# A triangular inverse inside a two-layer transformer kernel: levels 1 to 4 on compact 32-column blocks, four TensorE tiles at a time

## The chip, the cores and the metric

The kernel runs on one core of one Trainium2 chip, in one launch. The metric is the time of a whole execution on the device in microseconds (us), as the median of several runs; lower is better.

## The reference, cut to what matters

The program computes two layers of a 1024-wide transformer block on 256 tokens (a gated delta rule beside latent attention, feed-forwards), and behind it two layers of other mixers and feed-forwards. The change touches one step of the gated delta rule. Each layer has 8 heads of 128 channels, and a head's 256 tokens are cut into chunks:

```python
CHUNK = 64
m = jnp.where(strict, jnp.einsum('nbhid,nbhjd->nbhij', kb, kc) * decay, 0.0)
eye = jnp.eye(CHUNK, dtype=f32)
t_inv = lax.linalg.triangular_solve(eye + m, jnp.broadcast_to(eye, m.shape), left_side=True, lower=True)
u = t_inv @ (vc * bc[..., None])
w = t_inv @ (kb * jnp.exp(gcum)[..., None])
```

`m` is strictly lower triangular, so `eye + m` has an inverse that can be built from small blocks on the diagonal upwards. The kernel works on chunks of 128 tokens, not 64, which gives the same result: two chunks for each head, and so 16 inverses of 128 x 128 for each layer. All numbers are float32.

## The kernel before, in words

**Where the inverse stands.** `delta_rule` handles the heads in two groups `g` of four; with two chunks each, a group has 8 independent *units* `u`, all of which go through the inverse together. There are two groups for each of two layers, so `inverse(g, fill)` (L1026) is run four times in an execution: it begins at about 353, 422, 1176 and 1246 us. VectorE (DVE) first makes `MT`, the transposed and decayed product of keys with keys for the 8 units.

**The doubling.** `TI` holds the inverse of the blocks on the diagonal so far and `TTI` its transpose. At the start the blocks are 2 x 2 (`TTI = I - EBS[0]`, L2343). Level s (1 to 5) doubles the block's size. `EBS[s % 2]` is `MT` times a mask that leaves just the new off-diagonal blocks, with sign. TensorE forms X = EBS TI in banks 0 and 1 of PSUM; X is copied to `XB`; then `TTI X` and `X TTI` are *added* to the copies of TI and TTI that stay in PSUM (banks 2 and 3, banks 4 and 5; `start=False`), and both are copied out again. The last step (L1075 and `last_block`, L1085) joins the two 64 x 64 halves.

**Tiles.** All products of the five levels are done by `square_products` (L1028) as 64 x 64 x 64: unit u, rows 0 to 63 (`BLOCKS[0]`, low) and rows 64 to 127 (`BLOCKS[1]`, high) are two matmuls, on two tiles of the array with 64 rows and 64 columns each. A profile shows each float32 matmul as two weight loads and two matmul records, and those of two neighbouring tiles alternate. So 8 units x 2 halves are 32 records.

**Who copies.** ScalarE (ACT) copies the low half (L1484), DVE the high half (L2348), 64 partitions x 512 in one instruction. DVE also makes the mask product for the next level (L2355, 128 x 1024). In the first group of each layer DVE does a convolution between (L2030, L2034) and ACT a SiLU (L1418).

**Filler.** While ACT and DVE copy, TensorE must not stand still. `mixer_filler` (L963) hands out the tiles of large independent projections: `MIX_FILL` says how many tiles (of 128 x 128 weights and 256 columns, two records each, L976) stand at each point of the order. The points `ti0`, `level01` to `level05` are those of group 0, `ti1`, `level11` to `level15` of group 1. Sixteen tiles are a *job*, whose two outputs ACT moves from PSUM (`move`, L1422 to L1432) once TensorE has done the job's last tile. Within a level the order on TensorE is: wait, X (32 records), filler, wait, TTI X (32), X TTI (32), and then the next level's wait. The order on each engine is the program's order, and all waits are semaphores counted (`cnt.next`): `products_for_act` and `products_for_dve` from TensorE, `operands_of_act` and `operands_of_dve` to it. Between the first products and level 1 stand the products of keys and queries (L1051) and DVE's `QK` (L2352).

**Constants.** `kst` holds masks, seven of them of 128 columns for the levels. All but its first 128 columns are loaded once, behind the ninth weight slab.

Of the kernel before, what the change touches and what calls it, by code (L numbers as in the profile page):

```python
# [24 lines left out]
ALU = mybir.AluOpType  # L25
ACT = mybir.ActivationFunctionType
AXX = mybir.AxisListType.X

P = 128
# [18 lines left out]
MIX_FILL = dict(keys_early=3, keys=21, queries=14, decay0=24, ti0=1, level01=10, level02=10, level03=5, level04=5,  # L48
                level05=5, rb0=6, u00=5, state0=3, carry0=5, u10=3, decay1=26, ti1=1, level11=6, level12=6, level13=6,
                level14=6, level15=6, rb1=6, u01=5, state1=3, carry1=5, u11=3, out=9,  # L50
# [21 lines left out]
def ada_turns():  # L72
# [26 lines left out]
_CK = dict(ones=128, ident=128, cmask=512, bmask=512, upper=128, levels=7 * 128, rot=128, pick=128,  # L99
           freq=1)  # L100
# [29 lines left out]
CK, NK = columns(_CK)  # L130
# [25 lines left out]
def build(nc, wstream, astream, crow, xT, memT, pos, par1, par2, pars, const, outT):  # L156
    ctx = ExitStack()
    with ctx:
# [11 lines left out]
        kst = sb("kst", [P, NK])  # L170
# [24 lines left out]
        level = [kst[:, CK["levels"][0] + P * s:CK["levels"][0] + P * (s + 1)] for s in range(7)]  # L195
# [40 lines left out]
        TMP = 14336  # L236
# [5 lines left out]
        EBS = [area(TMP + 4096, 8, P), area(TMP + 9216, 8, P)]  # L242
# [62 lines left out]
        BLOCKS = (slice(0, 64), slice(64, P))  # L305

        def blocks_of(b, rows):

            return psum[rows, b].rearrange("p (u t) -> p u t", t=64)

# [200 lines left out]
        def _(pe):  # L511
# [514 lines left out]
            def inverse(g, fill):  # L1026

                def square_products(bank, lhs, rhs, blocks=(0, 1), signals=(products_for_act, products_for_dve), **flags):  # L1028
                    for u in range(8):
                        for r in blocks:  # L1030
                            rows = BLOCKS[r]
                            mm = pe.matmul(psum[rows, bank + r, 64 * u:64 * u + 64], lhsT=lhs(rows, u), rhs=rhs(rows, u),  # L1032
                                           skip_group_check=True, **{n: f(u) for n, f in flags.items()})
                            if u == 7:
                                mm.then_inc(signals[r], 1)

                def own(v):
                    return lambda rows, u: v[rows, u, rows]

                def unit(rows, u):  # L1040
                    return ident[rows, rows]

                opens = dict(start=lambda u: u == 0, stop=lambda u: False)
                adds = dict(start=lambda u: False, stop=lambda u: False)
                alone = dict(start=lambda u: True, stop=lambda u: True)

                pe.wait_ge(operands_of_dve, cnt.next("operands_of_dve"))
                square_products(2, own(TTI), unit, **opens)
                for u in range(8):
                    j, c = u // 2, u % 2  # L1050
                    mm = pe.matmul(psum[:, u // 4, u % 4 * P:(u % 4 + 1) * P],  # L1051
                                   lhsT=qkv[:, 8 + 4 * g + j, c * P:(c + 1) * P],
                                   rhs=qkv[:, 4 * g + j, c * P:(c + 1) * P], start=True, stop=True)
                mm.then_inc(products_for_dve, 1)
                for u in range(8):
                    for r, rows in enumerate(BLOCKS):
                        pe.matmul(psum[rows, 4 + r, 64 * u:64 * u + 64], lhsT=unit(rows, u), rhs=TTI[rows, u, rows],
                                  start=u == 0, stop=False, skip_group_check=True)
                fill(f"ti{g}")

                for s in range(1, 6):
                    pe.wait_ge(operands_of_act, cnt.next("operands_of_act"))
                    pe.wait_ge(operands_of_dve, cnt.next("operands_of_dve", 2 if s == 1 else 1))
                    square_products(0, own(EBS[s % 2]), own(TI), **alone)
                    fill(f"level{g}{s}")
                    pe.wait_ge(operands_of_act, cnt.next("operands_of_act", 1 if s == 1 else 2))
                    pe.wait_ge(operands_of_dve, cnt.next("operands_of_dve", 1 if s == 1 else 2))
                    square_products(2, own(TTI), own(XB), (0, 1) if s < 5 else (0,), **adds)
                    square_products(4, own(XB), own(TTI), **adds)

                pe.wait_ge(operands_of_act, cnt.next("operands_of_act"))
                pe.wait_ge(operands_of_dve, cnt.next("operands_of_dve"))
                low, high = BLOCKS
                for u in range(8):
                    mm = pe.matmul(psum[high, 3, 64 * u:64 * u + 64], lhsT=EBS[0][low, u, high], rhs=TI[low, u, low],  # L1075
                                   start=True, stop=True)
                mm.then_inc(products_for_act, 1)
# [209 lines left out]
        def _(act):  # L1287
# [114 lines left out]
            def mixer(layer):  # L1402
# [70 lines left out]
                for g in range(2):  # L1473
                    act.wait_ge(inputs_for_act, cnt.next("inputs_for_act"))
                    E(DT, DT, ACT.Exp)
                    E(eg, rows4[g][:, :, P:T], ACT.Exp).then_inc(functions_for_dve, 1)
                    move(f"decay{g}")
                    if g == 0:
                        silu(9)
                    low, high = BLOCKS  # L1480

                    def take(dst, bank, rows):
                        act.wait_ge(products_for_act, cnt.next("products_for_act"))
                        E(dst, blocks_of(bank, rows), ACT.Identity).then_inc(operands_of_act, 1)  # L1484

                    take(TI[low, :, low], 2, low)
                    move(f"ti{g}")
                    for s in range(1, 6):
                        take(XB[low, :, low], 0, low)
                        if g == 0 and s in (2, 3):  # L1490
                            silu(8 + s)
                        move(f"level{g}{s}")
                        take(TI[low, :, low], 2, low)
                        take(TTI[low, :, low], 4, low)
                    take(XB[high, :, low], 3, high)
# [149 lines left out]
        def _(dve):  # L1645
# [655 lines left out]
            def delta_rule(layer):  # L2301
# [3 lines left out]
                def lev(s):  # L2305
                    return level[s].unsqueeze(1).broadcast_to((P, 8, P))
# [7 lines left out]
                def product():  # L2314
                    dve.wait_ge(products_for_dve, cnt.next("products_for_dve"))

                convolve(layer, 8)
                for g in range(2):
# [21 lines left out]
                    TT(EBS[0], MT, lev(0), ALU.mult)  # L2340
                    D()
                    TT(TTI, I8, EBS[0], ALU.subtract).then_inc(operands_of_dve, 1)
                    TT(EBS[1], MT, lev(1), ALU.mult)  # L2343
                    low, high = BLOCKS

                    def take(dst, bank, rows):
                        product()
                        return V.tensor_copy(dst, blocks_of(bank, rows))  # L2348

                    take(TI[high, :, high], 3, high).then_inc(operands_of_dve, 1)  # L2350
                    product()
                    TT(QK, two(0), DT, ALU.mult).then_inc(operands_of_dve, 1)  # L2352
                    for s in range(1, 6):
                        take(XB[high, :, high], 1, high).then_inc(operands_of_dve, 1)
                        last = TT(EBS[(s + 1) % 2], MT, lev(s + 1), ALU.mult)  # L2355
                        if g == 0 and s in (1, 2):
                            convolve(layer, 9 + s)
                        if s < 5:
                            take(TI[high, :, high], 3, high).then_inc(operands_of_dve, 1)
                        else:  # L2360
                            last.then_inc(operands_of_dve, 1)
                        take(TTI[high, :, high], 5, high).then_inc(operands_of_dve, 1)
                    take(TTI[low, :, high], 4, low)
# [542 lines left out]
def constants():  # L2906
# [6 lines left out]
    levels = []  # L2913
    for s in range(7):
        b = 2 << s
        new = (i[:, None] // b == i[None, :] // b) & (i[None, :] % b >= b // 2) & (i[:, None] % b < b // 2)
        levels.append(np.where(new, -1.0 if s else 1.0, 0.0))
    rot = np.zeros((P, P))
    for m in range(P):
        if m % 64 < 32:  # L2920
            rot[m + 32, m] = -1.0
        else:
# [4 lines left out]
                          i[None, :] >= i[:, None], *levels, rot, pick, freq[:, None]], 1).astype(np.float32)  # L2927
# [18 lines left out]
```

## Time and profile before

| | |
|---|---|
| median of 3 runs | 2652.08 us (2651.91 to 2652.47) |
| profiled execution, its own time | 2653.67 us |
| span of the profiled execution | 2651.5 us |
| mean granted TensorE clock | 0.997 of full speed |
| busy share: TensorE, DVE, ACT, GpSimd | 99%, 60%, 17%, 6% |
| matmul records of the four inverses (64*64) | 2176 of 17960 |

The span runs from the first to the last instruction; the execution's own time is about 2 us longer. A matmul's record lasts from its start to the modelled end, some 0.2 us of which overlap with those behind it, so a group's busy time says less than the distance between starts.

### The profile page before, as it was taken

Reading aid. Unit: us, or ns where it says so; the run is one execution under the profiler, and the core shown is the slowest. Engines: PE = TensorE matmul, PEld = TensorE weight load, DVE = VectorE, ACT = ScalarE, POOL = GpSimd, SP = SyncE. Lnnn points to the kernel's source line nnn. Section 1 sums busy time; section 2 is a strip of 40 time slices with the busy share of each in tenths; the row PEclk is TensorE's granted clock in tenths of the full one; section 3 lists DMA queues with packets and bytes.
Section 4 is the critical chain, followed back from the end, with each engine's and each line's share of the span. In section 5 each row is a group of like instructions: output and inputs, shape, how many; then the busy total and the mean of one; then the engine's idle time right before and its main releaser. Section 6 shows DMA issues by size and latency. Waiting matters only on the chain.

```text
span 2651.5 us, 43071 instructions
## 1 busy us (share of the span) xinstructions
PE 2613.9 (99%) x17960; PEld 2360.4 (89%) x17960; DVE 1595.2 (60%) x3378; ACT 446.9 (17%) x857; POOL 160.3 (6%) x138
## 2 busy tenths in 40 slices
PE   9999999999999999999999999999999999999998
PEld 8899888788999999888878999987889998888998
DVE  4587675646677778675554666344358752324775
ACT  1011333221000100233321100013110011211000
POOL 0000000000330430000000330000000000000000
PEclk9999999999999999999999999999999999999999
DMA  9887422527446556532345444443344444343442
GB/s 379 307 334 268 163 104 81 198 96 244 170 160 253 200 207 223 214 128 81 141 154 199 155 164 175 151 166 112 111 144 158 159 160 177 116 143 120 158 154 94
DMA packets 74450, 458.88 MB, mean 173 GB/s; under 512 B 8308, under 2 KB 9216, under 8 KB 28176
## 3 DMA queue, kind: packets, MB, share of 16 engines
q1 hardware_dynamic: 73120, 449.28, 46.3%
q0 software_dynamic: 1136, 6.86, 0.7%
q8 instruction: 141, 2.31, 0.3%
q14 instruction: 53, 0.43, 0.1%
HBM read 455.01 MB, written 1.09 MB: 172 GB/s over the span
## 4 chain that ended last, share of the span: by engine, by line
PE 94%; DVE 4%; DMA 1%; DVEq 1%; issue 0%; ACT 0%; ACTq 0%
PE psum L548 20%; PE psum L780 14%; PE psum L722 14%; PE psum L629 9%; PE psum L976 8%; PE psum L828 4%; PE psum L1032 3%; PE psum L605 2%; PE psum L735 2%; PE psum L664 2%; PE psum L996 2%; PE psum L651 2%; PE psum L924 1%; PE psum L951 1%; DMA aring<-astream 1%; DVE aring L1912 1%
## 5 line engine op out<-in xcount | busy, mean ns | idle before, releaser
L548 PE MATMUL psum<-h,ring 128*128 128x256 f32 x1536 | 335.0, 379 | 1.4 <-DVE arena L1886 0.8
L548 PEld LDWEIGHTS psum<-h,ring 128*128 128x128 f32 x1536 | 291.1, 190 | 43.1 <-ACT arena L1460 1.7
L780 PE MATMUL psum<-arena 128*128 128x128 f32 x2112 | 249.7, 275 | 1.2 <-DVE arena L1786 1.2
L780 PEld LDWEIGHTS psum<-arena 128*128 128x128 f32 x2112 | 242.6, 192 | 1.4 <-DVE arena L1786 1.4
L629 PE MATMUL psum<-aring,ring 128*128 128x256 f32 x1088 | 237.3, 379 | 1.7 <-issue 1.7
L976 PE MATMUL psum<-h,ring 128*128 128x256 f32 x1024 | 235.4, 383 | 0.0
L629 PEld LDWEIGHTS psum<-aring,ring 128*128 128x128 f32 x1088 | 205.8, 190 | 29.9 <-issue 2.4
L976 PEld LDWEIGHTS psum<-h,ring 128*128 128x128 f32 x1024 | 189.9, 190 | 30.2 <-issue 4.9
L780 PE MATMUL psum<-arena,ring 128*128 128x128 f32 x1584 | 191.6, 275 | 0.0
L780 PEld LDWEIGHTS psum<-arena,ring 128*128 128x128 f32 x1584 | 184.3, 192 | 0.2
L722 PE MATMUL psum<-arena 128*128 128x128 f32 x1440 | 170.6, 275 | 0.0
L722 PEld LDWEIGHTS psum<-arena 128*128 128x128 f32 x1440 | 165.6, 192 | 0.0
L548 PE MATMUL psum<-arena,ring 128*128 128x256 f32 x720 | 157.9, 380 | 1.0 <-DVE arena L2148 1.0
L1912 DVE SCALAR_TENSOR_TENSOR aring<-aring,condb 128x1024 f32<-128x1024 f32 x128 | 153.0, 1220 | 8.5 <-DMA aring<-astream 7.7
L548 PEld LDWEIGHTS psum<-arena,ring 128*128 128x128 f32 x720 | 136.1, 190 | 24.3 <-issue 4.7
L1300 ACT ACTIVATE sq<-x 128x512 f32<-128x512 f32 x48 | 30.3, 631 | 591.8 <-DVEq L1889 381.7
L722 PE MATMUL psum<-h,ring 128*128 128x128 f32 x960 | 117.0, 275 | 0.0
L477 POOL TENSOR_TENSOR arena<-ring 128x512 f32<-128x512 f32 x60 | 77.1, 1285 | 645.2 <-PE psum L584 426.3
L722 PEld LDWEIGHTS psum<-h,ring 128*128 128x128 f32 x960 | 112.2, 192 | 0.2
L664 PE MATMUL psum<-h,ring 128*128 128x256 f32 x448 | 96.9, 379 | 0.3 <-DVE arena L1972 0.3
L664 PEld LDWEIGHTS psum<-h,ring 128*128 128x128 f32 x448 | 85.0, 190 | 12.2 <-issue 0.6
L1783 DVE TENSOR_TENSOR arena<-ring 128x512 f32<-128x512 f32 x66 | 45.6, 691 | 75.4 <-PE psum L780 74.3
(463 smaller groups left out, 3726.0 us busy)
## 6 DMA issues: line engine op xcount, KB each, us to landing
ring<-wstream SPq DMA_DIRECT2D x349, 1024.0 KB, 4.9
aring<-astream SPq DMA_DIRECT2D x128, 512.0 KB, 4.9
arena<-astream SPq DMA_DIRECT2D x16, 512.0 KB, 18.3
arena<-wstream SPq DMA_DIRECT2D x3, 1024.0 KB, 20.2
arena<-decays POOLq DMA_DIRECT2D x2, 1024.0 KB, 5.4
sq<-decays POOLq DMA_DIRECT2D x2, 1024.0 KB, 4.7
kst<-const SPq DMA_DIRECT2D x1, 1216.5 KB, 7.6
x<-xT SPq DMA_DIRECT2D x1, 1024.0 KB, 4.9
```

The costliest lines, as they stand in the source:

```text
L477: nc.gpsimd.tensor_tensor(new[:, 0], w[:, 2], w[:, 3], ALU.add)
L548: mm = pe.matmul(out, lhsT=tile_at(at[0] % RING, t), rhs=rhs(k), start=k == 0, stop=k == kt - 1)
L605: mm = pe.matmul(psum[:, bank + bk, c * P:(c + 1) * P], lhsT=w, rhs=v, start=m == 0 and name in ("M1", "M5"), stop=m == 3, skip_group_chec ...
L629: mm = pe.matmul(psum[:, s % 4, n * T:(n + 1) * T], lhsT=tile_at(slot, 8 * n + 4 * (k % 2) + k // 2), rhs=rhs(k), start=k == 0, stop=k == ...
L651: mm = pe.matmul(psum[:, s, n * T:(n + 1) * T], lhsT=slab[:, t * P:(t + 1) * P], rhs=h[:, k], start=k == 0 and n == 0, stop=k == KD - 1, s ...
L664: mm = pe.matmul(psum[:, s % 4, n * T:(n + 1) * T], lhsT=tile_at(at[0] % RING, n * KD + k), rhs=h[:, k], start=k == 0, stop=k == KD - 1)
L722: mm = pe.matmul(out, lhsT=w, rhs=v, start=m == 0 and name in ("M1", "M5"), stop=m == 3, skip_group_check=True)
L780: mm = pe.matmul(out, lhsT=w, rhs=v, start=m == 0 and name in ("M1", "M5", "M3", "M4"), stop=m == NF // 2 - 1, skip_group_check=True)
L828: mm = pe.matmul(psum[:, memory_bank(kind, job), a * T:(a + 1) * T], lhsT=w, rhs=v, start=k == 0, stop=k == KD - 1)
L976: mm = pe.matmul(psum[:, 6 + job % 2, n * T:(n + 1) * T], lhsT=tile_at(i % RING, f % TPS), rhs=h[:, k], start=k == 0, stop=k == KD - 1)
L1032: mm = pe.matmul(psum[rows, bank + r, 64 * u:64 * u + 64], lhsT=lhs(rows, u), rhs=rhs(rows, u), skip_group_check=True, **{n: f(u) for n, f ...
L1912: STT(out=w, in0=w, scalar=1.0, in1=condb[:], op0=ALU.mult, op1=ALU.mult, accum_out=sums[:, b:b + 1]).then_inc(ada_used, 1)
```

## The change

The inverse's blocks are held compactly, and a matmul makes 32 columns instead of 64. `QUADS` are the four groups of 32 partitions. The four diagonal 32 x 32 blocks of a unit stand one below the other in a 128 x 32 area (`TC` for TI, `XC` for X). A product takes 64 rows of weights and of data (`BLOCKS[b // 2]`) and 32 columns of weights (`QUADS[b]`), on a tile of 64 rows and 32 columns; one of its two 32-row halves is zero in one operand. Four such tiles stand side by side in the array, so a product of all units is 8 x 4 = 32 matmuls, 64 records, where it was 32 records.

- Levels 1 to 4 (which build blocks of up to 32 x 32) use this form. `NEAR` (`MT` within blocks of 32, negated) is made once; the mask of a level is applied when X is copied, by DVE, in two instructions of 64 x 256 (`level[s - 1]`).
- Level 5 joins 32 x 32 blocks with tiles of 32 rows and 32 columns, straight from `MT`, 16 matmuls and then 24; the last two joins keep their 64 x 64 form.
- ACT copies TC for both halves (two instructions of 64 x 256) and TTI for two of the four blocks (two of 32 x 256); DVE copies TTI for the other two.
- Each level's `TTI X` and `X TTI` are now followed by a filler point of its own, `turn`, of one tile in levels 1 to 4. The order of a level is: wait, X (64 records), filler `level`, wait, TTI X (64), X TTI (64), filler `turn`. The filler tiles of a group's inverse add up to the same as before (36 and 31).
- `kst` shrinks by 480 columns.

```diff
-MIX_FILL = dict(keys_early=3, keys=21, queries=14, decay0=24, ti0=1, level01=10, level02=10, level03=5, level04=5,
-                level05=5, rb0=6, ..., decay1=26, ti1=1, level11=6, level12=6, level13=6,
-                level14=6, level15=6, rb1=6, ...
+MIX_FILL = dict(keys_early=3, keys=21, queries=14, decay0=24, ti0=1, level01=8, turn01=1, level02=8, turn02=1, level03=7, turn03=1,
+                level04=6, turn04=1, level05=2, rb0=6, ..., decay1=26, ti1=1, level11=7, turn11=1, level12=6, turn12=1, level13=6, turn13=1, level14=5,
+                turn14=1, level15=2, rb1=6, ...
-                def square_products(bank, lhs, rhs, blocks=(0, 1), signals=(products_for_act, products_for_dve), **flags):
+                def quad_products(bank, lhs, rhs, signals, start, stop):
                     for u in range(8):
-                        for r in blocks:
-                            rows = BLOCKS[r]
-                            mm = pe.matmul(psum[rows, bank + r, 64 * u:64 * u + 64], lhsT=lhs(rows, u), rhs=rhs(rows, u),
...
+                        for b in range(4):
+                            mm = pe.matmul(psum[QUADS[b], bank + b // 2, 32 * u:32 * u + 32], lhsT=lhs(b, u),
+                                           rhs=rhs(b, u), start=start(u), stop=stop, skip_group_check=True)
+                            if u == 7 and b in signals:
+                                mm.then_inc(signals[b], 1)
...
                 pe.wait_ge(operands_of_dve, cnt.next("operands_of_dve"))
-                square_products(2, own(TTI), unit, **opens)
+                quad_products(2, own(TTI), units, {3: products_for_act}, lambda u: u == 0, False)
...
+                quad_products(4, units, own(TTI), {}, lambda u: u == 0, False)
+                fill(f"ti{g}")
+
+                for s in range(1, 5):
+                    pe.wait_ge(operands_of_act, cnt.next("operands_of_act"))
+                    if s == 1:
+                        pe.wait_ge(operands_of_dve, cnt.next("operands_of_dve"))
+                    quad_products(0, own(NEAR), compact(TC), {3: products_for_dve}, lambda u: True, True)
+                    fill(f"level{g}{s}")
+                    if s > 1:
+                        pe.wait_ge(operands_of_act, cnt.next("operands_of_act"))
+                    pe.wait_ge(operands_of_dve, cnt.next("operands_of_dve", 1 if s == 1 else 2))
+                    quad_products(2, own(TTI), compact(XC), {3: products_for_act}, lambda u: False, False)
+                    quad_products(4, compact(XC), own(TTI), {1: products_for_act, 3: products_for_dve}, lambda u: False, False)
+                    fill(f"turn{g}{s}")
...
+                fill(f"level{g}5")
+                pe.wait_ge(operands_of_act, cnt.next("operands_of_act", 2))
+                pe.wait_ge(operands_of_dve, cnt.next("operands_of_dve", 2))
+                for u in range(8):
+                    out = slice(256 + 32 * u, 288 + 32 * u)
+                    for r in range(2):
+                        even, odd = QUADS[2 * r], QUADS[2 * r + 1]
+                        if r == 0:
+                            mm = pe.matmul(psum[odd, 2, out], lhsT=TTI[odd, u, odd], rhs=XC[odd, u], start=True, stop=True,
+                                           skip_group_check=True)
...
+                        mm = pe.matmul(psum[even, 4 + r, out], lhsT=XC[odd, u], rhs=TTI[odd, u, odd], start=True,
+                                       stop=True, skip_group_check=True)
...
+                    for s in range(5):
+                        if s == 4:
+                            take((TQ[QUADS[0], :, 0:32], quads_of(2, QUADS[0])), (TQ[QUADS[1], :, 32:64], quads_of(2, QUADS[1])),
+                                 (TC[QUADS[2]], quads_of(3, QUADS[2])))
+                        else:
+                            take(*[(TC[rows], quads_of(2 + r, rows)) for r, rows in enumerate(BLOCKS)])
+                        if s > 0:
+                            take(own(0), own(1))
...
+                    for s in range(1, 5):
+                        product()
+                        for r, rows in enumerate(BLOCKS):
+                            last = TT(XC[rows], quads_of(r, rows), all_units(level[s - 1][rows]), ALU.mult)
+                        last.then_inc(operands_of_dve, 1)
                         if g == 0 and s in (1, 2):
                             convolve(layer, 9 + s)
...
+                        product()
+                        for b in (2, 3):
+                            last = V.tensor_copy(TTI[QUADS[b], :, QUADS[b]], quads_of(5, QUADS[b]))
+                        last.then_inc(operands_of_dve, 1)
```

## Rows read from the trace of the kernel before

**Rows 1.** The page: busy time of the engines; the chain that ended last, by engine.

```profile
PE 2613.9 (99%) x17960; PEld 2360.4 (89%) x17960; DVE 1595.2 (60%) x3378; ACT 446.9 (17%) x857; POOL 160.3 (6%) x138
...
PE 94%; DVE 4%; DMA 1%; DVEq 1%; issue 0%; ACT 0%; ACTq 0%
```

**Rows 2.** Busy time by stretch: the first two inverses; then clock, DMA share, GB/s.

```profile
352.61:390.01 37.40, 37.40 (x633) 32.84 (x632) 24.10 (x37) 12.27 (x21) 0.00 (x0) 1.00 0.23 81
421.78:457.02 35.24, 35.24 (x623) 30.94 (x622) 17.77 (x21) 10.63 (x18) 0.00 (x0) 1.00 0.23 80
```

**Rows 3.** The critical chain through the first inverse: start us, us, what.

```profile
352.68 1.08 PE psum L1032 x32
353.76 1.98 PE psum L1051 x16
...
356.82 0.63 PE psum L976 x2
...
363.04 3.14 PE psum L1032 x96
366.18 4.51 PE psum L976 x20
...
387.19 1.95 PE psum L1032 x47
389.13 0.95 PE psum L1075 x16
...
395.40 0.89 PE psum L1116 x8
```

**Rows 4.** Timeline: X of level 3 to level 4, with ACT's and DVE's copies.

```profile
376.12 3.21 PE L1032 MATMUL psum<-arena 64*64 64x64 f32 x96
377.30 0.59 ACT L1484 ACTIVATE arena<-psum 64x512 f32<-64x512 f32 x1 [2.35 <-PE psum L1032]
...
378.28 0.69 DVE L2348 COPY arena<-psum 64x512 f32<-64x512 f32 x1 [0.24 <-PE psum L1032]
379.26 2.02 PEld L976 LDWEIGHTS psum<-h,ring 128*128 128x128 f32 x10
```

**Rows 5.** Timeline: the first four, then eight weight loads of four 32-column tiles (L843).

```profile
305.32 0.13 PEld L843 LDWEIGHTS psum<-sq,kst 128*32 128x32 f32 x4 [0.33 <-DVE sq L2225]
305.32 0.64 PE L843 MATMUL psum<-sq,kst 128*32 128x512 f32 x4
...
305.32 0.16 PEld L843 LDWEIGHTS psum<-sq,kst 128*32 128x32 f32 x8 [0.33 <-DVE sq L2225]
...
305.32 1.07 PE L843 MATMUL psum<-sq,kst 128*32 128x512 f32 x8
```

**Rows 6.** Line L843 from 305 to 306.5 us: ns min/median/max, first and last start.

```profile
L843 PEld LDWEIGHTS psum<-sq,kst x8: 106/108/109, 305.3 to 305.4; 128*32 128x32 f32 x8
L843 PE MATMUL psum<-sq,kst x8: 592/605/617, 305.3 to 305.8; 128*32 128x512 f32 x8
```

**Rows 7.** Timeline: copies, products and a convolution of other sizes on ACT and DVE.

```profile
355.78 1.23 DVE L2352 TENSOR_TENSOR arena<-psum,arena 128x1024 f32<-128x1024 f32 x1 [1.25 <-PE psum L1051]
...
361.15 2.79 DVE L2034 SCALAR_TENSOR_TENSOR arena<-arena,p 128x256 f32<-128x256 f32 x6
...
391.58 1.02 ACT L1497 ACTIVATE arena<-psum 128x1024 f32<-128x1024 f32 x1 [0.87 <-PE psum L1109]
392.50 0.59 ACT L1498 ACTIVATE arena<-psum 128x512 f32<-128x512 f32 x1
```

**Rows 8.** Line L1032 over the whole span: who waited for it (us, times).

```profile
  ACT arena L1484: 95.8, 64
  DVE arena L2348: 55.9, 60
```

More of the change, by code:

```diff
@@ L98 @@
            lq1=64, lk1=64, lq2=64, lk2=64)
-_CK = dict(ones=128, ident=128, cmask=512, bmask=512, upper=128, levels=7 * 128, rot=128, pick=128,
+_CK = dict(ones=128, ident=128, cmask=512, bmask=512, upper=128, pairs=128, near=128, levels=4 * 32, unit=32, rot=128, pick=128,
            freq=1)
@@ L194, in build @@
         ones, ident, upper, rot, pick = K("ones"), K("ident"), K("upper"), K("rot"), K("pick")
-        level = [kst[:, CK["levels"][0] + P * s:CK["levels"][0] + P * (s + 1)] for s in range(7)]
+        level = [kst[:, CK["levels"][0] + 32 * s:CK["levels"][0] + 32 * (s + 1)] for s in range(4)]
         now = [0]
@@ L305, in build, with quads_of @@
         BLOCKS = (slice(0, 64), slice(64, P))
+        QUADS = tuple(slice(32 * b, 32 * b + 32) for b in range(4))
         def blocks_of(b, rows):
             return psum[rows, b].rearrange("p (u t) -> p u t", t=64)
+        def quads_of(b, rows, at=0):
+            return psum[rows, b, at:at + 256].rearrange("p (u t) -> p u t", t=32)
         def bank(b, n=1, w=512):
@@ L1054, in inverse @@
                 mm.then_inc(products_for_dve, 1)
-                for u in range(8):
[L1056 to L1069, printed above, removed]
+                quad_products(4, units, own(TTI), {}, lambda u: u == 0, False)
@@ new lines, in inverse @@
+                pe.wait_ge(operands_of_act, cnt.next("operands_of_act"))
+                for u in range(8):
+                    for r, t in enumerate((TQ[QUADS[0], u, 0:32], TC[QUADS[2], u])):
+                        even, odd = QUADS[2 * r], QUADS[2 * r + 1]
+                        mm = pe.matmul(psum[odd, r, 32 * u:32 * u + 32], lhsT=MT[even, u, odd], rhs=t,
+                                       start=True, stop=True, skip_group_check=True)
+                        if u == 7:
+                            mm.then_inc((products_for_act, products_for_dve)[r], 1)
@@ L1480, in mixer, with take, own @@
                     low, high = BLOCKS
-                    def take(dst, bank, rows):
+                    def take(*parts, scale=1.0):
                         act.wait_ge(products_for_act, cnt.next("products_for_act"))
[L1484 to L1489, printed above, removed]
+                        for dst, src in parts:
+                            last = E(dst, src, ACT.Identity, scale=scale)
+                        last.then_inc(operands_of_act, 1)
+                    def own(b):
+                        return TTI[QUADS[b], :, QUADS[b]], quads_of(4 + b // 2, QUADS[b])
+                    for s in range(5):
[6 more added lines that the diff above has]
+                            take(own(0), own(1))
                         if g == 0 and s in (2, 3):
                             silu(8 + s)
[L1492 to L1495, printed above, removed]
+                        move(f"turn{g}{s}" if s else f"ti{g}")
+                        if s < 4:
+                            move(f"level{g}{s + 1}")
+                    take((XC[QUADS[1]], quads_of(0, QUADS[1])), scale=-1.0)
+                    move(f"level{g}5")
+                    take((TQ[QUADS[1], :, 0:32], quads_of(2, QUADS[1], 256)))
+                    take((TTI[QUADS[0], :, QUADS[1]], quads_of(4, QUADS[0], 256)))
+                    take((XB[high, :, low], blocks_of(3, high)), scale=-1.0)
                     act.wait_ge(products_for_act, cnt.next("products_for_act"))
@@ L2339, in delta_rule @@
                     D()
[L2340 removed]
+                    TT(PAIRS, MT, all_units(K("pairs")), ALU.mult)
                     D()
[L2342 to L2343 removed]
+                    TT(TTI, I8, PAIRS, ALU.subtract).then_inc(operands_of_dve, 1)
+                    TT(NEAR, MT, all_units(K("near")), ALU.mult)
                     low, high = BLOCKS
[L2346 to L2348 removed]
@@ L2364, in delta_rule @@
+                    V.tensor_copy(TTI[low, :, high], blocks_of(4, low))
                     dve.wait_ge(functions_for_dve, cnt.next("functions_for_dve"))
@@ L2912, in constants @@
     never, always = np.full((P, P), NEG), np.zeros((P, P))
-    levels = []
-    for s in range(7):
+    pairs = (i[:, None] // 2 == i[None, :] // 2) & (i[None, :] % 2 == 1) & (i[:, None] % 2 == 0)
+    near = np.where(i[:, None] // 32 == i[None, :] // 32, -1.0, 0.0)
+    levels, q = [], np.arange(32)
+    for s in range(1, 5):
         b = 2 << s
-        new = (i[:, None] // b == i[None, :] // b) & (i[None, :] % b >= b // 2) & (i[:, None] % b < b // 2)
-        levels.append(np.where(new, -1.0 if s else 1.0, 0.0))
+        levels.append((i[:, None] % 32 // b == q[None, :] // b) & (i[:, None] % b >= b // 2) & (q[None, :] % b < b // 2))
+    unit = i[:, None] % 32 == q[None, :]
     rot = np.zeros((P, P))
```

52 lines of the change are left out of this document (25 added, 27 removed).

## The prediction

> **What bounds the kernel now.** I read the page first. TensorE is busy 99% of the span and is 94% of the chain that ended last [rows 1]: the kernel's time is the time of TensorE's stream, and work that leaves DVE or ACT is worth nothing. Then the windows over the inverses: in 352.61 to 390.01 us TensorE is busy all 37.40 us, at granted clock 1.00 (the 2.4 GHz level), DMA at 0.23 of its share [rows 2]. So there is no idle time for the change to remove; it has to make TensorE's own work shorter. The other three inverses are the same pieces with 36 or 31 filler tiles between. Third the chain through the first inverse, piece by piece [rows 3], which gives prices. Fourth the timeline round one level, to see who copies when [rows 4]. Last the one place where this kernel already runs four tiles of 32 columns side by side, L843 [rows 5, 6]. ACT and DVE wait 151.7 us in sum for the inverse's products [rows 8], so they have room.
>
> **Prices on TensorE.** A lone 64 x 64 tile (L1075, one half only) takes 0.95 us for 16 records, 59.4 ns each; a 128 x 128 product with 128 columns (L1116) takes 0.89 / 8 = 111 ns [rows 3]. From 64 to 128 columns of weights and of data the record grows by 52 ns, 0.81 ns for each column. Two tiles together: 32 records in 1.08 us, which is 16 x 59.4 = 0.95 us and 0.13 us before the dense work behind them starts [rows 3]. So two neighbouring tiles run fully in parallel, 29.7 ns a record, and what sets the pace is each tile's own cycle, not the pair. Two dense records take 0.63 us where they stand alone and 4.51 / 20 = 0.226, or by difference (4.51 - 0.63) / 18 = 0.216, in a row [rows 3]: 0.20 us more than 2 x 0.216. A burst of small tiles between dense ones thus costs 0.13 + 0.20 = 0.33 us besides its records. The burst of 96 takes 3.14 us = 48 x 59.4 (2.85) + 0.13 + 0.16: the last 0.16 us is the wait of the next level's X for DVE's copy, which ends at 378.28 + 0.69 [rows 3, 4].
>
> **Before, one inverse.** Its 544 records are 512 in paired tiles (15.2 us) and 32 on a lone tile (1.9 us): 17.1 us. Check: the window 37.40 less L1051 (1.98) less 72 dense records (15.5) leaves 19.9 us; 17.1 + 8 bursts x 0.33 (2.6) + 4 waits x 0.16 (0.6) is 20.3. Good to 0.4 us.
>
> **After, one inverse: what is not shown, and its bounds.** Tiles of 64 rows and 32 columns with 32 columns of data occur nowhere. By the 0.81 ns a column the cycle of one tile is 59.4 - 26 = 33.4 ns. Do four of them run in parallel? L843 says yes for column tiles: the first four loads last 0.13 us in all, the shortest 0.106, so the fourth starts 0.024 us after the first; the eighth ends at 0.16 and lasts 0.109, so it starts at 0.051, 27 ns behind the fourth, its own tile's first [rows 5, 6]. Four loads of 32 columns at once cost the time of one, 27 ns, and the four matmuls start within 0.02 us of each other [rows 5]. Row tiles in parallel are shown by the inverse itself. So I take one *round* of four records at 33.4 ns, 8.4 ns a record; the floor is the 27 ns of the load. The upper bound for a record is what before shows sustained, 29.7 ns.
>
> The records: start 2 x 64, levels 1 to 4 with 4 x 192, level 5 with 32 (two tiles) and 48 (three tiles), together 976; in rounds 32 + 192 + 16 + 16 = 256. 256 x 33.4 ns = 8.55 us, and L1075 as before 0.95: 9.5 us. **Records: 9.5 - 17.1 = -7.6 us.**
>
> **Bursts.** The `turn` points cut each of four bursts in two: 12 for 8. **+4 x 0.33 = +1.3 us.** The filler tiles themselves are the same number.
>
> **Waits.** Level 1's X waits for `QK`: DVE can start it once L1051 is done and needs 1.23 us [rows 7]; TensorE meanwhile does 16 rounds (0.53), a burst's edge and two dense records, 1.3 us: about even, +0.1. After `TTI X` of a level ACT makes two copies of 64 x 256. ACT's slope is (1.02 - 0.59) / 512, 0.84 ns an element [rows 7], so one is 0.59 - 0.22 = 0.37 and, a little overlapped, two are 0.65 to 0.75; with 0.25 for the drain and the semaphores the copy is there 0.9 to 1.0 us after the last record of `TTI X`. TensorE is then at `X TTI` (0.53), one filler tile (0.43) and a burst's edges (0.33): 1.3 us. Covered, also in level 4 with three ACT copies (1.2). The wait of 0.16 us in the four old bursts goes, -0.6. DVE's masked copies, two of 256 elements at about 0.47 (2.79 / 6 [rows 7]), lie under 5 to 8 filler tiles (2.2 us and more); the convolution behind them (2.79 us and a little more [rows 7]) ends about when `turn` starts and is wanted only after it. The mask products L2355 leave DVE, which saves nothing. New and uncovered: in level 5 the last join (L1075's successor) follows directly on the 48 records and waits for ACT's copy of the 32 x 256 block, 0.25 + 0.37 = +0.65. **Waits together: +0.15 us.** If ACT's copy of 256 elements cost as much as one of 512 (0.59), two more waits of 0.2 to 0.4 us would come in every level: a rival below.
>
> **The rest.** 480 fewer constant columns are 0.24 MB less in one transfer while TensorE is busy: nothing. A job's copy by ACT (`move`) now stands once between `TTI X` copies; it falls under the 1.3 us. Behind the inverse nothing changes, and transfers (0.23 of their share) will keep up with a stream that arrives 6 us earlier.
>
> **Sum.** -7.6 + 1.3 + 0.15 = -6.1 us for each of four inverses, -24.5 us. Profiled execution 2653.7 (span 2651.5): 2629. It was 1.6 us above the median of the runs shown, 2652.1, from which I forecast 2627.6, rounded to **2628 us**.
>
> Break-even is where 976 records cost 6.1 us more than at 8.4 ns: 14.6 ns a record.
>
> **Rival 1: the cycle doesn't shrink with the columns.** Then a round of four costs 59.4 ns as a round of two did: 256 x 59.4 ns + 0.95 = 16.2 us, -0.9 + 1.3 + 0.15 = +0.5 us an inverse, +2 us: **2654 us**. For it: no row has so few columns. Against: 111 against 59 ns for half the columns is still nearly in proportion, and loads of 32 columns turn round in 27 ns [rows 3, 5]. Chance 0.12. The Trainium skill has this rule against the change, in "TensorEngine Tiling (Array Packing)", section Instruction Overhead: a matmul carries some 60 cycles, one with a free dimension of 1 takes as long as one of 60, and a tiling factor isn't to be taken from a dimension that is already small. Read as a floor on columns, it gives this rival's time; read as cycles it does not bite if a float32 record takes two cycles a column, which would fit the 0.81 ns a column seen here.
>
> **Rival 2, the other side: the stream of instructions can't keep up.** TensorE must be fed two records (a load and a matmul) every 8.4 ns; before shows 29.7 ns sustained, and only short runs faster: eight loads and four matmuls start within 0.05 us [rows 5]. If the sequencer delivers a pair in, say, 20 ns, 976 x 11.6 ns = +11.3 - 6.1 = +5.2 us an inverse, +21: **2673 us**; at the bound of 29.7 ns it is 4 x (20.8 - 6.1) = +59, 2711 us. It decides above 14.6 ns a record; a queue that runs ahead during the filler would soften it. Against: in bursts of 96 records the two tiles show no sign of starving. Chance 0.15. The Trainium skill ("TensorE: Matmul & The Clock Gate", Part 1) says that starts of matmuls never lie closer than about 25 ns, however few columns; by that the sum would be about +10 us an inverse, 2691 us. Rows 5 contradict it across tiles: four matmuls start within 0.02 us; no row here tells for a long stream.
>
> **Rival 3: new waits eat part.** ACT now has up to five small copies in each `turn`, and TensorE passes from X to copy to X with one filler tile. If small copies cost 0.55 us each instead of 0.37, each turn waits some 0.4 us and level 5 about 0.8 more: 2.5 us an inverse, **2638 us**. For it: fixed costs weigh more in small instructions. Against: the slope above. Chance 0.15.
>
> **Numbers.** The forecast has 0.58. Its own range: rounds at 27 ns give another 4 x 256 x 6.4 ns = -6.6 us, 2621; 10 ns a record gives +6, 2634. Up to the other cases: from 2621 to 2656 lie the forecast, rivals 1 and 3, 0.85 together, less tails of 0.05. Faster by over 0.2% (5.3 us, about what a measurement can tell from no change): forecast and rival 3, 0.73. Rival 1 is within 0.2%: 0.12. Slower is rival 2: 0.15.
>
> **What the profile after would show.** Right: bursts of 64 records in about 0.53 + 0.13 us, of 128 in 1.1 to 1.2; the window of the first inverse about 31.3 us with the same filler; no waits of the small records for ACT before level 2, 3, 4; one of about 0.65 us before the 64 x 64 join. Rival 1: 64 records in 0.95 + 0.13. Rival 2: a burst of 128 that costs far more than twice one of 64, its starts evenly spaced. Rival 3: idle time before the small loads, released by ACT. The prediction would be wrong most of all through the price of a record: every nanosecond on it is 3.9 us.

## The result: slower by 0.38%

| | before | after |
|---|---|---|
| median of 5 runs each | 2652.47 us (2651.91 to 2655.62) | 2663.43 us (2660.77 to 2664.57) |
| profiled execution, its own time | 2653.67 us | 2660.77 us |
| ratio, 95% interval | | 1.0038 (1.0024 to 1.0051) |

The forecast was 2628 us; the kernel became 11 us slower instead of 24 us faster, and the range (to 2656) missed it. The page of the profile after, as in [rows 1], and the row of the queue that carries instructions:

```profile
PE 2599.1 (98%) x19752; PEld 2338.3 (88%) x19752; DVE 1563.4 (59%) x3374; ACT 442.6 (17%) x881; POOL 160.9 (6%) x138
...
q8 instruction: 155, 2.54, 0.4%
...
PE 91%; DVE 4%; DMA 2%; issue 1%; DVEq 1%; ACT 1%; ACTq 0%
```

and that last kind of row in the kernel before (queue: packets, MB, share of 16 engines):

```profile
q8 instruction: 141, 2.31, 0.3%
```

TensorE is less busy and the kernel is longer: idle time has come in. The timeline of TensorE's matmuls in the first inverse shows where (start us, us, ..., idle before and what ended it):

```profile
353.02 0.76 PE L1038 MATMUL psum<-kst,arena 64*32 64x32 f32 x64
353.71 2.05 PE L1056 MATMUL psum<-arena 128*128 128x128 f32 x16
...
361.50 1.31 PE L1038 MATMUL psum<-arena 64*32 64x32 f32 x128
362.74 0.70 PE L983 MATMUL psum<-h,ring 128*128 128x256 f32 x2
363.37 0.26 PE L1038 MATMUL psum<-arena 64*32 64x32 f32 x7
365.45 0.69 PE L1038 MATMUL psum<-arena 64*32 64x32 f32 x57 [1.83 <-issue]
...
371.60 0.66 PE L1038 MATMUL psum<-arena 64*32 64x32 f32 x52
375.81 0.43 PE L1038 MATMUL psum<-arena 64*32 64x32 f32 x12 [3.55 <-issue]
376.17 6.03 PE L983 MATMUL psum<-h,ring 128*128 128x256 f32 x14
382.13 1.32 PE L1038 MATMUL psum<-arena 64*32 64x32 f32 x128
```

Two things stand here together. The small matmuls are as cheap as forecast: 64 records from 353.02 to 353.71, 0.69 us, 128 from 361.50 to 362.74, 1.24 us (forecast 0.66, and 1.1 to 1.2). But TensorE stops in the *middle* of a product, after 7 records of X of level 2 and after 52 of X of level 3, for 2.0 and 3.8 us from start to start. No semaphore of the program stands there; "issue" says that the profile shows nothing that it waited for. And behind the second stop 14 dense records take 5.96 us, not 3.0. The windows tell why (PE, PEld, DVE, ACT, POOL busy; clock; DMA share; GB/s):

```profile
353.02:394.36 41.34, 34.59 (x1081) 27.94 (x1080) 15.42 (x36) 11.31 (x27) 0.00 (x0) 0.92 0.23 79
...
363.45:365.40 1.95, 0.18 (x7) 0.07 (x7) 0.30 (x1) 0.38 (x2) 0.00 (x0) 1.00 0.00 0
...
372.10:375.80 3.70, 0.16 (x17) 0.05 (x4) 0.00 (x0) 0.63 (x1) 0.00 (x0) 0.88 0.52 215
376.20:382.10 5.90, 5.90 (x16) 4.51 (x14) 0.84 (x2) 0.00 (x0) 0.00 (x0) 0.53 0.01 3
```

The same piece took 37.40 us before [rows 2]. During the stops ACT and DVE have next to nothing to do either: they are not what is waited for. In the stop of 3.7 us the granted clock begins to fall (0.88 over it), behind it it is at the lower level (1.2 GHz; 0.53 over the window), and dense work pays double until it rises.

**What the stops have in common.** TensorE's instructions come by queue 8 in packets of 16 KB: 155 of them for 39,504 loads and matmuls, 141 for 35,920 before, one for about 256 (a load and a matmul record are an instruction each). Counting all records that TensorE has in the trace from its start, its semaphore instructions too (39,802), the ten long stops in the inverses come after record 4545, 5057, 5825, 7617, 8385, 19905, 20673, 21697, 22465 and 23233. Each is 193 more than a multiple of 256; such a place is called a block's *edge* below. They last 0.96 to 4.30 us, 21.1 us in sum, and before each of them ends a packet of queue 8 has begun 2.25 to 2.65 us earlier. That gave theory A: TensorE has used up its block of 256 instructions before the next is there. The rivals were B, it waits for ACT or DVE, and C, the sequencer's own rate.

The same count, block by block, tells which blocks are followed by a stop. In this trace TensorE goes through twelve blocks in under 3 us of running (the time from a block's first record to its last): 1.9 to 2.5 us each. Ten of them are followed by the ten stops; the packet for the block after the other two had begun 0.9 us before they were entered. The one before the first stop can be read in the timeline above: from 361.57 to 363.43 us, nearly all of `TTI X` and `X TTI` (128 pairs, that is 256 instructions), a filler tile and 7 records of X. In the kernel before, the shortest block in the inverses runs for 6.1 us.

### The profile page after: what moved, and what is told of

The parts are those of the page before. It is cut to its first block, busy times and chain, and to the rows that moved or that the text cites. A ratio compares the mean times of both kernels' runs of the same rounds, so it can differ in the third digit from the quotient of the medians.

```text
span 2659.0 us, 46651 instructions
## 1 busy us (share of the span) xinstructions
PE 2599.1 (98%) x19752; PEld 2338.3 (88%) x19752; DVE 1563.4 (59%) x3374; ACT 442.6 (17%) x881; POOL 160.9 (6%) x138
## 4 chain that ended last, share of the span: by engine, by line
PE 91%; DVE 4%; DMA 2%; issue 1%; DVEq 1%; ACT 1%; ACTq 0%
PE psum L555 20%; PE psum L729 14%; PE psum L787 14%; PE psum L636 9%; PE psum L983 8%; PE psum L835 4%; PE psum L612 2%; PE psum L742 2%; PE psum L1003 2%; PE psum L658 2%; DMA aring<-astream 2%; PE psum L1038 1%; PE psum L671 1%; PE psum L931 1%; DVE aring L1954 1%
## 5 line engine op out<-in xcount | busy, mean ns | idle before, releaser
L555 PE MATMUL psum<-h,ring 128*128 128x256 f32 x1536 | 335.0, 379 | 1.4 <-DVE arena L1928 0.8
L983 PE MATMUL psum<-h,ring 128*128 128x256 f32 x1024 | 245.6, 391 | 0.0
L671 PE MATMUL psum<-h,ring 128*128 128x256 f32 x448 | 96.9, 379 | 0.3 <-DVE arena L2014 0.3
```

Source lines behind the costliest of these rows:

```text
L555: mm = pe.matmul(out, lhsT=tile_at(at[0] % RING, t), rhs=rhs(k), start=k == 0, stop=k == kt - 1)
L671: mm = pe.matmul(psum[:, s % 4, n * T:(n + 1) * T], lhsT=tile_at(at[0] % RING, n * KD + k), rhs=h[:, k], start=k == 0, stop=k == KD - 1)
L983: mm = pe.matmul(psum[:, 6 + job % 2, n * T:(n + 1) * T], lhsT=tile_at(i % RING, f % TPS), rhs=h[:, k], start=k == 0, stop=k == KD - 1)
```

## Experiments

**A burst by itself.** The disputed cost alone, in the kernel before:

```diff
                 pe.wait_ge(operands_of_dve, cnt.next("operands_of_dve"))
+                if not padded:
+                    padded.append(1)
+                    for n in range(80):
+                        for b in range(4):
+                            rows = slice(32 * b, 32 * b + 32)
+                            pe.matmul(psum[rows, 0, 32 * (n % 8):32 * (n % 8) + 32], lhsT=ident[rows, 0:32],
+                                      rhs=ident[rows, 0:32], start=True, stop=True, skip_group_check=True)
```

> The kernel before, with 320 extra matmuls of 32 rows x 32 columns x 32 on four tiles (640 weight loads, 640 matmul records) in one burst ahead of the first inverse; they write a PSUM region that is overwritten and change nothing else. Theory A (instruction blocks: TensorE's instructions arrive in transfers of 16 KB, 256 instructions, and one is only asked for when the block before it is entered, so 256 instructions can't be used up in less than some 5 to 6 us): the burst starts at 8.4 ns a pair, stops dead after the blocks in hand, about 250 to 500 instructions, and then once every 256 instructions, four or five stops of 3 to 5 us, 18 to 25 us in all instead of 5.4, with an instruction transfer that starts about 2.3 us before each stop ends; the granted clock may fall to 0.5. Theory B (TensorE waits for ACT's or DVE's copies in the changed kernel): the burst has nothing to wait for and takes 5.4 us. Theory C (the sequencer's own rate): evenly spaced records, no stops, at any price per pair.

Measured 2669.1 us, in a single run. The burst in the timeline:

```profile
350.91 2.19 PE L1055 MATMUL psum<-kst 32*32 32x32 f32 x236
355.14 1.29 PE L1055 MATMUL psum<-kst 32*32 32x32 f32 x128 [2.04 <-issue]
358.59 1.93 PE L1055 MATMUL psum<-kst 32*32 32x32 f32 x128 [2.17 <-issue]
362.32 1.93 PE L1055 MATMUL psum<-kst 32*32 32x32 f32 x128 [1.80 <-issue]
366.05 0.53 PE L1055 MATMUL psum<-kst 32*32 32x32 f32 x20 [1.80 <-issue]
```

236 pairs run without a break at 8.5 ns each; then come stops, and between two stops exactly 128 matmuls and 128 loads: 256 instructions. The four come after record 4289, 4545, 4801 and 5057, again 193 above a multiple of 256. A and not B (nothing here is waited for) nor C (no even spacing). The stops were shorter than I wrote, 2.0 to 2.4 us from start to start, and so was the whole, 15.6 us (350.91 to 366.51): a block takes 3.45 to 3.73 us at the fastest. That time has two parts: the packet for the next block begins 1.0 to 1.2 us after the first record of the block just entered, and TensorE goes on 2.3 to 2.7 us after the packet's start. From the second stop on the clock is at its lower level, where a row of 128 pairs lasts 1.93 us instead of 1.29.

**The same burst with weights on the way.** The condition becomes `if g == 1 and not padded`, which moves the burst ahead of the second inverse, where 1 MB of weights is being loaded.

> The burst of 320 small matmuls (1280 records) again in the kernel before, but ahead of the second inverse, some 1 us after a job of filler ends and frees a weight slab, so that 1 MB of weights is on its way while TensorE's instructions are fetched. In the first burst the four stops were 2.0 to 2.4 us with no weights on the way. Theory A1 (the transfer of instructions also queues behind the weights): the first or second stop is 2 to 4 us longer than those four, its instruction transfer starts only when the weights' packets end, the later stops are 2.0 to 2.4 us again. Theory A2 (a block's delay is TensorE's own, the weights don't matter): four stops of 2.0 to 2.4 us.

```profile
424.52 1.60 PE L1055 MATMUL psum<-kst 32*32 32x32 f32 x167
430.36 1.93 PE L1055 MATMUL psum<-kst 32*32 32x32 f32 x128 [4.24 <-issue]
434.09 1.92 PE L1055 MATMUL psum<-kst 32*32 32x32 f32 x128 [1.80 <-issue]
437.55 1.93 PE L1055 MATMUL psum<-kst 32*32 32x32 f32 x128 [1.53 <-issue]
441.00 1.43 PE L1055 MATMUL psum<-kst 32*32 32x32 f32 x89 [1.52 <-issue]
```

The single run took 2675.58 us. The first stop is 4.24 us, the other three 1.5 to 1.8. Windows over the burst's start, the first and the second stop:

```profile
424.70:425.90 1.20, 1.20 (x162) 1.20 (x155) 0.00 (x0) 0.00 (x0) 0.00 (x0) 1.00 1.03 177
426.00:430.30 4.30, 0.13 (x15) 0.01 (x1) 0.00 (x0) 0.00 (x0) 0.00 (x0) 0.89 0.45 187
432.10:434.00 1.90, 0.19 (x16) 0.05 (x4) 0.00 (x0) 0.00 (x0) 0.00 (x0) 0.50 0.00 0
```

The packet of instructions begins at 428.15 us, when the weights' packets have ended. So A1: a block's transfer also queues behind a weight slab, and that adds some 2.5 us here. In the changed kernel the stop at 372.1 is of this kind (DMA share 0.52 in it), the one at 363.4 follows on a share of 0.77 from 360.0 to 363.4. Its three longest stops, 3.75, 3.76 and 4.30 us, are all so: their packets begin 3.3, 3.3 and 3.9 us after the block before is entered, within 0.4 us of the end of the weights' packets, where those of the other seven begin after 0.7 to 1.7 us.

**Shifted by half a block.** The changed kernel with 32 small matmuls (128 instructions) more ahead of the first inverse, by the same lines with `range(8)`.

> The changed kernel with 32 small matmuls more (128 instructions, half a block) ahead of the first inverse alone; they write a PSUM region that is overwritten. Theory A: every stop in the inverses now comes 128 instructions earlier in the program, that is, at other places of the levels (the first one in the burst for the turn of level 1 or 2 instead of X of level 2), and always where the count of TensorE's records is 449 more than a multiple of 256; the sum of stops stays 12 to 25 us. Theory B: the stops stay at X of levels 2 and 3 in the first inverse.

The single run took 2655.95 us. TensorE in levels 2 to 4 of the first inverse:

```profile
369.20 1.23 PE L1040 MATMUL psum<-arena 64*32 64x32 f32 x118
370.98 0.28 PE L1040 MATMUL psum<-arena 64*32 64x32 f32 x10 [0.55 <-issue]
...
377.60 0.50 PE L1040 MATMUL psum<-arena 64*32 64x32 f32 x35
379.44 0.45 PE L1040 MATMUL psum<-arena 64*32 64x32 f32 x29 [1.35 <-issue]
...
382.60 0.94 PE L1040 MATMUL psum<-arena 64*32 64x32 f32 x87
```

X of level 2 runs through now; the stops have moved to other products (the first near the end of the turn of level 2), and 14 stops of over 0.6 us stand at a block's edge, at 193 + a multiple of 256, with 18.2 us in sum (one of them, 0.64 us, is as long as the wait for ACT at the same place of the other traces and may be that). None reaches 2 us: half a block's shift alone takes the three longest away. Their place is the count of instructions, not the step of the program. B is out.

**More work for the same instructions.** Up to four zero-weight dense matmuls are put among the filler of each level:

```diff
+                        if point[:5] == "level" and point[6] < "5" and more > 0 and k < KD - 1:
+                            more -= 1
+                            pe.matmul(psum[:, 6 + job % 2, n * T:(n + 1) * T], lhsT=K("cmask")[:, 256:384],
+                                      rhs=h[:, k], start=False, stop=False)
```

> The changed kernel with four dense matmuls more (128 x 128 x 256, zero weights added to a filler output, so that no value changes) in each of the filler points of levels 1 to 4: 64 in all, 0.43 us each, +27.6 us of TensorE work. Theory A: each block of instructions now lasts longer, so most of the 21 us of stops and the 5 to 10 us of half clock go: 2660 to 2672 us, within 10 us of the changed kernel. Theory B or C, or a cost in the tiles themselves: the full 27.6 us come on top, 2688 to 2691 us.

2682.43 us, ratio 1.0104 (1.0087 to 1.0121): 19 us over the changed kernel, where 27.6 us of work came on top. It lies between the ranges of A and of its rivals. The direction is A's, the size is not: the trace, of the fastest of the four runs (2676.49 us), still has eight stops at block edges, 14.4 us in sum for 21.1. By the prices a level of 214 pairs, 428 instructions, now takes 7.0 us, and a block 4.2 us on average, above the 3.5 to 3.7 us of the burst. But the average is not what counts. The extra work stands in the filler of the level; the 128 pairs of `TTI X` and `X TTI` still follow each other, and seven of the eight stops follow a block that ran for 1.2 to 2.8 us. Three of the eight have a packet that began late, as weights' packets ended; four others, of 1.3 to 1.6 us, have one that began 0.8 us after the block was entered.

**Fewer instructions, dearer matmuls.** The contrast that counts: X as 64 x 64 tiles on the compact blocks (the weights are block-diagonal, so one matmul makes two blocks below each other), 32 records for 64.

```diff
+                def pair_products(bank, lhs, rhs, signals, start, stop):
+                    for u in range(8):
+                        for r, rows in enumerate(BLOCKS):
+                            mm = pe.matmul(psum[rows, bank + r, 32 * u:32 * u + 32], lhsT=lhs[rows, u, rows],
+                                           rhs=rhs[rows, u], start=start(u), stop=stop, skip_group_check=True)
+                    mm.then_inc(signals[3], 1)
-                    quad_products(0, own(NEAR), compact(TC), {3: products_for_dve}, lambda u: True, True)
+                    pair_products(0, NEAR, TC, {3: products_for_dve}, lambda u: True, True)
```

> The changed kernel with X of levels 1 to 4 made by tiles of 64 rows and 64 columns on the compact blocks: 16 matmuls (32 records) instead of 32 (64 records). 160 pairs a level instead of 192. By the prices so far X costs 0.95 us instead of 0.53, +1.7 us an inverse, +6.7 in all. Theory A: fewer instructions, so the stops and the half clock (some 21 and 5 to 10 us of the changed kernel) fall to about half: 2648 to 2658 us. Theory C (stops not from the number of instructions): 2670 us.

2647.91 us, ratio 0.998 (0.997 to 0.9991): 15 us under the changed kernel, though its matmuls take 7 us longer by the prices. The trace, of a run of 2641.58 us, has six stops, 5.9 us. The 11 runs spread from 2640.33 to 2653.15 us, far more than the kernel before in its own runs (2651.05 to 2655.44), and the spread goes with the granted clock: 0.998 in the three fastest, 0.993 to 0.995 in the five slowest. What lowers it in some runs only, no trace here shows.

With TTI X in the same form too (`pair_products(2, TTI, XC, ...)`), 128 pairs a level:

> As the run before, and TTI X of levels 1 to 4 with 64-column tiles as well: 128 pairs a level. Records cost +3.4 us an inverse over the changed kernel, +13.4 in all, the change of tile shape inside a turn perhaps 0.15 us more. Theory A: a block of instructions now lasts over 5 us; no stops but the odd one behind a weight slab: 2643 to 2650 us, faster than before and than the changed kernel, though its matmul records take longer. Theory C: 2677 us.

2644.03 us, ratio 0.9968 (0.9956 to 0.9979). A turn of it in the timeline:

```profile
364.76 1.12 PE L1046 MATMUL psum<-arena 64*64 64x32 f32 x32
365.81 0.76 PE L1038 MATMUL psum<-arena 64*32 64x32 f32 x64
366.50 0.70 PE L983 MATMUL psum<-h,ring 128*128 128x256 f32 x2
```

TTI X takes 1.05 us for 32 records where 64 of the narrow ones take about half of that, and there is no idle time on the way to the other tile shape. Those 32 records have 32 columns of data and take what 32 with 64 columns of data took before (1.08 us, [rows 3]): on these tiles half the data columns saved nothing, the price went with the columns of the weights. In the inverses no stop at a block's edge exceeds 0.6 us, and no block runs for less than 3.1 us. The slower products make the faster kernel.

**Without the turn's filler tile.** `turn01=0` and its like, the tile given to the level.

> The changed kernel with the filler tile of each turn moved to the level's filler: four bursts fewer an inverse (-1.3 us), but X follows on X TTI at once and waits about 0.5 us for ACT's copy in each level, and 192 pairs stand in a row. Without instruction blocks: +0.5 us an inverse, 2665 us. Theory A: the same number of instructions per level, used up in a shorter stretch, with the longer filler behind it: stops of about the same sum, 2660 to 2670 us. If turns are what costs: under 2655 us.

2671.85 us, ratio 1.0071 (1.0056 to 1.0085), 8 us above the changed kernel and above both ranges. Its nine stops at block edges have 22.0 us in sum, hardly more than the changed kernel's 21.1 us; X waits for ACT's copy twelve times, 0.3 us each; four of the stops instead of three exceed 3.5 us; and in six stretches of 3.4 to 13.7 us (44 us together, 14 in the changed kernel's inverses) the clock is at its lower level. Against "if turns are what costs", fewer bursts don't help; that the lower clock makes up the 8 us is argued, not tested.

**Level 5 alone** in the kernel before, the rest untouched: the changed kernel's two products of 32 x 32 tiles on the uncompacted TI and XB, as many instructions as before.

> The kernel before with level 5 alone in the changed form: 32 x 32 tiles, 16 and 24 matmuls where it had 16 and 24 of 64 x 64, no level-5 mask; levels 1 to 4 and all filler as before. The number of TensorE instructions is unchanged. Theory A: the block of instructions round level 5 is used up 1 us faster but is followed by long filler, so no stops: records -1.8 us an inverse, +0.45 us for the wait of the last join, -1.2 to -1.4 us an inverse, 2647 us. If small 32 x 32 tiles or the mode change cost more than thought: 2652 us or above.

2647.42 us, ratio 0.9975 (0.9964 to 0.9985), and no stops:

```profile
383.15 0.69 PE L1082 MATMUL psum<-arena 32*32 32x32 f32 x32
383.77 2.42 PE L982 MATMUL psum<-h,ring 128*128 128x256 f32 x10
...
387.28 1.14 PE L1106 MATMUL psum<-arena 64*64 64x64 f32 x16 [0.45 <-ACT arena L1515]
```

This part of the change is a gain by itself, some 6 us against its own runs of the kernel before (2653.47), with the new wait for ACT's copy in front of the last join, as forecast.

**The best version, and one more step.** The value transposes, which wait for nothing, moved into that last wait.

> The kernel with 64-column tiles for X and TTI X, and the eight transposes of the values moved ahead of the last join of the inverse, into its wait of 0.64 us for ACT's copy. The wait goes (-0.64 us), a burst's edges come (+0.33): -0.3 us an inverse, -1 us, 2643 us. If the transposes only push the join, whose copy ACT and then last_block wait for, the wait comes back behind it: no change, 2644 us.

> The kernel with 64-column tiles for X and TTI X of levels 1 to 4 once more, beside the run before on the same chip: 2642 to 2646 us. Theory A: no stop of over 0.5 us at a block's edge in its trace, or one at most, behind a weight slab.

Run together: 2642.34 us (0.9957; 0.9944 to 0.9971) with the transposes moved, 2643.32 (0.9963; 0.9951 to 0.9976) without. The wait is gone as meant, but 1 us is inside the spread of both (2640.86 to 2644.89 and 2643.24 to 2645.24): not settled. Neither trace has a stop of over 0.5 us at a block's edge. Both beat the kernel before by 10 us and the changed one by 20.

## Why the prediction was wrong, step by step

- **What bounds the kernel, bursts, level 5's wait: right.** Twelve bursts; the wait before the last join is 0.64 us from start to start, forecast 0.65; no matmul of levels 2 to 4 waits for ACT.
- **A record at 8.4 ns, four tiles in parallel: right.** A burst of 64 takes 0.69 us, and 236 pairs in a row ran at 8.5 ns each. Rival 1 is out. The rule of the Trainium skill in "TensorEngine Tiling (Array Packing)", section Instruction Overhead, read as a floor on columns, does not hold here. Nor does its 25 ns between the starts of matmuls (the Trainium skill, "TensorE: Matmul & The Clock Gate", Part 1) hold across tiles.
- **The step that failed: the sum has no term for getting the instructions.** I counted records as time alone. 192 pairs a level are 384 instructions, and with the filler some 412 in 5.3 us, a block of 256 in 3.3 us on average. Within a level it is worse: my own price for a burst of 128 pairs, 1.1 to 1.2 us, was the price of a whole block, and the blocks that hold it ran for 1.9 to 2.5 us. In the changed kernel a block followed by a stop took, from its first record to the next block's, 3.0 to 4.0 us at the seven shorter stops and 5.6 to 6.2 us at the three behind a slab: 21.1 us of standstill in all. Before, a level has 216 instructions in 5.93 us, a block in 7.0. "Transfers (0.23 of their share) will keep up" looked at the weights alone; the transfer that mattered was 0.4% of the queues' time, and it is its delay, not its size, that counts.
- **Rival 2 came true in direction, not in mechanism.** It had 0.15, priced as an even rate of the sequencer, with the remark that "in bursts of 96 records the two tiles show no sign of starving". True, and no evidence: 96 pairs are 192 instructions, less than one block. Its time, 2673 us, was nearer than the forecast.
- **The ledger** of the two profiled executions: -24.5 us by the forecast, +21.1 of stops, and the lower clock: 14 dense records in 5.96 us, 12 in 4.48 and 12 in 4.31 against 0.216 each come to +6.5. That makes +3.1; measured is +7.1. One more stretch of low clock at 1416 us, behind a wait of 1.8 us for DVE that stands in the kernel before as well, is 2.8 us of the rest, by the distance of the same matmuls in the two traces. That the clock fell there in one trace and not in the other is not explained, and 1.2 us stay open.

That block edges are where TensorE stops, and that weights lengthen the stop, is shown. In both bursts the packet for the next block begins 1.0 to 1.2 us after a stop has ended, not earlier; what fills that time, and the 1.2 to 1.4 us from the packet's end to TensorE's next record, stays open. The changed kernel was not run with its weights held back.

The Trainium skill, "Runtime: NRT & Kernel Launch", section Instruction fetch mechanics, says that an engine's instructions are fetched in blocks of 256, the next while the current one is executed, and that crossing a block's edge is mostly hidden. The traces agree on the 256. An edge is hidden in the kernel before, whose blocks in the inverses run for 6.1 us or more, and in that with two wide products, where they run for 3.1 us or more; behind blocks of 1.9 to 2.5 us it costs 1.0 to 4.3 us.

## What to carry to other kernels

Instructions are a resource of their own on TensorE. Before splitting matmuls into smaller, cheaper ones, count the instructions (a float32 matmul shows four) and look for the shortest stretch that holds 256 of them, not for the average: here stretches of 3.1 us and more cost nothing in the kernel with two wide products, those of 1.9 to 2.5 us cost 21 us in ten stops, and work added elsewhere in the level (an average of 4.2 us) took only a third of that away. If the gain needs a shorter one, take the larger tile: half the instructions of two products at double the price each won 20 us. A stop "<- issue" in the middle of a loop that has no wait is the sign; look at its record's count modulo 256.

## What the runs showed that was not expected

- One block of 256 instructions every 3.45 to 3.73 us in a burst, and 4.24 us of standstill where 1 MB of weights was on the way.
- Four tiles of 32 columns sustain 8.5 ns a pair over 236 pairs, and tile shapes 64*64 and 64*32 follow each other with no gap (1.05 and 0.69 us for their records).
- The three stops of 3.75 to 4.30 us in the changed kernel were each followed by dense work at the lower clock: 14 records in 5.96 us (granted clock 0.53), 12 in 4.48 and 12 in 4.31, where full speed needs 0.216 us each. None of the seven shorter ones was.
- ACT's copies of 256 columns (two of 64 partitions, two of 32) cost 0.39 us each in a row of four (1.55 us), close to the 0.37 worked out.
